# Gathering the rows of an expert layer by pairs of experts into two small buffers, and an eighth weight slot in place of the sorted array

## The reference, cut to what matters

```python
for i in range(DEPTH):                                  # DEPTH = 2
    h = rmsnorm(x, norm_mix[i])
    x = x + mixer(h, ...)                               # layer 0: sparse attention; layer 1: latent attention
    h = rmsnorm(x, norm_ffn[i]).reshape(512, 1024)
    x = x + hier_moe(h, ...)

def hier_moe(x2, ...):                                  # 512 tokens of 1024
    grp = argmax(softmax(x2 @ w_group + b_group))       # 1 of 8 groups
    top_p, top_i = top_k(softmax(logits of that group), 2)
    expert_id = grp * 8 + top_i                         # 2 of 64 experts for each token
    # rows sorted by expert: 1024 assignments, 16 for a mean expert
    y = (silu(xb @ w_gate[e]) * (xb @ w_up[e])) @ w_down[e]      # w_gate, w_up: 1024x256, w_down: 256x1024
    return for each token the weighted sum of its two rows of y
```

## Time and profile before

| what | value |
|---|---|
| median of 3 runs | 1631.71 us (1630.49 to 1633.06) |
| the profiled execution's own time | 1633.28 us |
| its span (first to last instruction) | 1631.5 us |
| TensorE busy | 1447.4 us, 89% |
| VectorE busy | 605.4 us, 37% |
| mean granted TensorE clock | 0.996 |
| experts, first up product of expert 0 to that of expert 60 | layer 0: 445.8 to 865.3 us; layer 1: 1160.3 to 1579.7 us |
| bytes moved by DMA | 480.67 MB, mean 295 GB/s |

### The profile page before, as it was taken

How to read it: one execution, slowest core, us unless ns; L and a number is a source line. 1 busy time by engine, 2 the same in 40 slices (tenths; PEclk the granted TensorE clock), 3 DMA queues, 4 the chain that set the end, 5 groups by cost and what they waited for, 6 DMA issues and landing times.

```text
span 1631.5 us, 24179 instructions
## 1 busy us (share of the span) xinstructions
PE 1447.4 (89%) x8991; PEld 903.8 (55%) x8991; DVE 605.4 (37%) x1517; ACT 341.0 (21%) x983; POOL 245.7 (15%) x290
## 2 busy tenths in 40 slices
PE   8999999999999988787878999999999977777785
PEld 3655466655566655454555555655666655555453
DVE  2145677752532221222213556423522222222225
ACT  2122377741110000000001345412100000000000
POOL 1122100000211111111112233000211111111112
PEclk9999999999999999999999999999999999999998
DMA  7115140026689999999999501473899999999997
GB/s 289 51 52 206 52 155 1 2 115 235 246 340 428 429 429 429 429 430 429 429 429 422 201 1 78 181 297 116 334 390 428 429 429 427 429 431 429 429 430 296
DMA packets 44373, 480.67 MB, mean 295 GB/s; under 512 B 11034, under 2 KB 11562, under 8 KB 24656
## 3 DMA queue, kind: packets, MB, share of 16 engines
q1 hardware_dynamic: 28144, 450.17, 65.9%
q0 software_dynamic: 15008, 25.37, 4.4%
q10 hardware_dynamic: 1152, 4.19, 0.6%
HBM read 461.33 MB, written 47.19 MB: 312 GB/s over the span
## 4 chain that ended last, share of the span: by engine, by line
PE 58%; DMA 32%; DVE 6%; issue 2%; ACT 1%; DVEq 0%; another core or an unknown queue 0%; POOL 0%; SPq 0%
DMA sb_arena<-moe_w 32%; PE ps L1173 12%; PE ps L1368 7%; PE ps L1583 7%; PE ps L1182 6%; PE ps L1689 2%; PE ps L1719 2%; PE ps L1704 2%; PE ps L1549 2%; PE ps L1409 2%; PE ps L1437 2%; PE ps L1433 1%; PE ps L1490 1%; PE ps L1520 1%; PE ps L1617 1%
## 5 line engine op out<-in xcount | busy, mean ns | idle before, releaser
L1173 PE MATMUL ps<-sb_arena,sb_x_block 128*64 128x256 f32 x4096 | 472.6, 383 | 91.5 <-DMA sb_arena<-moe_w 88.8
L1173 PEld LDWEIGHTS ps<-sb_arena,sb_x_block 128*64 128x64 f32 x4096 | 419.1, 197 | 198.6 <-issue 130.6
L1182 PE MATMUL ps<-sb_arena,sb_hidden_space 128*64 128x512 f32 x1024 | 247.9, 605 | 44.1 <-ACT sb_hidden_space L898 44.1
L768 POOL DMA_INDIRECT expert_rows<-sb_y_sb,sb_row_now x124 | 132.5, 1069 | 746.5 <-DVE sb_y_sb L1955 642.5
L1954 DVE COPY sb_row_now<-sb_row_of 128x1 uint32 (+1 forms) x124 | 19.1, 154 | 598.2 <-PE ps L1182 588.2
L898 ACT COPY sb_hidden_space<-ps 128x128 f32<-128x128 f32 x128 | 34.2, 267 | 755.8 <-PE ps L1248 755.8
L1182 PEld LDWEIGHTS ps<-sb_arena,sb_hidden_space 128*64 128x64 f32 x1024 | 62.1, 136 | 141.2 <-issue 73.1
L1368 PE MATMUL ps<-sb_sorted_rows,sb_arena 128*128 128x512 f32 x256 | 114.6, 594 | 2.1 <-DVE sb_arena L2199 1.3
L1965 DVE TENSOR_TENSOR sb_x_block<-sb_sorted_rows,sb_moe_gain 128x512 f32<-128x512 f32 x124 | 85.9, 693 | 25.0 <-issue 20.7
L1955 DVE COPY sb_y_sb<-ps 128x512 f32<-128x512 f32 x124 | 84.4, 681 | 0.0
L1368 PEld LDWEIGHTS ps<-sb_sorted_rows,sb_arena 128*128 128x128 f32 x256 | 46.9, 190 | 51.4 <-issue 48.8
(11 more groups left out here) (308 smaller groups left out, 1506.3 us busy)
## 6 DMA issues: line engine op xcount, KB each, us to landing
sb_arena<-moe_w SPq DMA_DIRECT2D x116, 3072.0 KB, 38.2
sb_arena<-moe_w SPq DMA_DIRECT2D x10, 2048.0 KB, 7.4
sb_arena<-moe_w SPq DMA_DIRECT2D x16, 1024.0 KB, 6.0
sb_sorted_rows<-nsa_w_group SPq DMA_DIRECT2D x2, 2048.0 KB, 13.2
sb_arena<-nsa_w_group SPq DMA_DIRECT2D x2, 2048.0 KB, 7.6
sb_sorted_rows<-nsa_w_out SPq DMA_DIRECT2D x1, 4096.0 KB, 13.9
kept_rows<-sb_arena SPq DMA_DIRECT2D x8, 512.0 KB, 4.9
token_rows<-sb_arena ACTq DMA_DIRECT2D x8, 512.0 KB, 2.7
```

Source lines behind the costliest of these rows:

```text
L768: pool.indirect_dma_start(out=ys_dram.rearrange("r (j n) -> (r j) n", j=2), out_offset=bass.IndirectOffsetOnAxis(ap=row_now[:, u:u + 1], a ...
L1173: last = nc.tensor.matmul(ps[j * BLOCK:(j + 1) * BLOCK, bank, 0:2 * P].rearrange("p (g n) -> p g n", g=2), x_rows[:, :, k], weights[:, 0:2 ...
L1182: last = nc.tensor.matmul(ps[j * BLOCK:(j + 1) * BLOCK, 2, :], hidT[:, c * BLOCK:(c + 1) * BLOCK], weights[:, 2, c * D + j * 512:c * D + ( ...
```

## The change

- `sorted_rows` no longer holds the rows. Its first part is weight slot 7 (`SLOTS = ARENA + 1 = 8`), its next part two buffers of 128 rows (`pair_rows`), each for one pair of experts: the 64 ranks of the even expert on partitions 0 to 63, those of the odd one on 64 to 127.
- Weight slot 7 is loaded by a third when the output projection has ended (`out_done`), and by two thirds after the last parts of slots 6 and 5.
- The list of tokens is by pair and rank: `token_of[p, q]` is the token of rank p % 64 of expert 2q + p // 64. Ranks come from the counting matmuls without `start`, tile by tile, and the one-hot matmuls of the first three tiles run during the routing. A missing rank gives 1000, out of bounds, and nothing is fetched for it.
- There are 32 indirect gathers of 128 descriptors of 4 KB instead of 8. The first two are issued when the list is ready. The gather of pair q + 2 waits for the turn of both blocks of pair q (the buffer) and stands in POOL's order between the row writes of expert 2q - 1 and expert 2q.
- TensorE turns the 64 rows of one expert with 8 transposes (`turn_block(n + 2)`) at the head of the iteration for expert n, ahead of `up(n + 1)`; an even one waits for its gather. `deal_block` reads the PSUM bank. The 16 copies into `xsT` go.
- The places in the sorted order (`start` plus rank) and the table for extra blocks are worked out after the first gathers; the router of the next layer is fetched after that table and ahead of the gather of pair 2.
- With over 64 rows for one expert, the extra blocks fetch their rows one by one. Neither layer's inputs need it.

```diff
-SLOTS = 7
+ARENA = 7
+SLOTS = ARENA + 1
...
-        xsT = sorted_rows[:, :].rearrange("p (n k) -> p n k", k=KD)
+        pair_rows = sorted_rows[:, SLOT:SLOT + 2 * D].rearrange("p (i n) -> p i n", i=2)
...
+        def slot_space(l, u):
+
+            return places(l, u) if u < ARENA else sorted_rows[:, 0:SLOT]
...
+                sp.wait_ge(out_done, OUT_PARTS * (l + 1))
+                part(ARENA, ARENA, 0, 1).then_inc(weights_loaded[ARENA], 16)
                 sp.wait_ge(last_rows_sent, 32 * (l + 1))
                 sp.wait_ge(logits_done, TILES * (l + 1))
                 part(RING + 2, RING + 2, 1, 3).then_inc(weights_loaded[RING + 2], 16)
                 part(RING + 1, RING + 1, 1, 2).then_inc(weights_loaded[RING + 1], 16)
+                part(ARENA, ARENA, 1, 3).then_inc(weights_loaded[ARENA], 16)
...
+                def gather(pair, j, tokens):
+                    pool.indirect_dma_start(
+                        out=pair_rows[:, j, :], out_offset=None, in_=h_dram,
+                        in_offset=bass.IndirectOffsetOnAxis(ap=tokens, axis=0),
+                        bounds_check=S - 1, oob_is_err=False).then_inc(pair_landed[j], 16)
+
+                pool.wait_ge(out_done, OUT_PARTS * (l + 1))
+                step(pool.memset(pair_rows, 0.0))
                 pool.wait_ge(token_ready, l + 1)
                 pool.wait_ge(first_rows_sent, 32 * (l + 1))
                 pool.wait_ge(last_rows_sent, 32 * (l + 1))
-                for c in range(CHUNKS):
-                    pool.indirect_dma_start(
-                        out=xs_in(c), out_offset=None, in_=h_dram,
-                        in_offset=bass.IndirectOffsetOnAxis(ap=token_of[:, c:c + 1], axis=0)).then_inc(rows_landed[c], 16)
+                for j in range(2):
+                    gather(j, j, token_of[:, j:j + 1])
 
                 pool.wait_ge(tables_ready, l + 1)
...
+                def send(i, u):
+                    pool.wait_ge(y_ready, i * 2 + (l * SENT + u + 1))
+                    pool.sem_inc(y_seen, 1)
+                    pool.indirect_dma_start(
+                        out=ys_dram.rearrange("r (j n) -> (r j) n", j=2),
+                        out_offset=bass.IndirectOffsetOnAxis(ap=row_now[:, u:u + 1], axis=0),
+                        in_=y_sb[:, u, :], in_offset=None, bounds_check=2 * ROWS - 1, oob_is_err=False
+                    ).then_inc(y_written[u], 16)
+
+                for j in range(2):
+                    pool.wait_ge(block_turned, base + 2 * j + 2)
+                    gather(j + 2, j, token_of[:, j + 2:j + 3])
                     for u in range(2):
-                        pool.wait_ge(y_ready, i * 2 + (l * SENT + u + 1))
+                        send(j, u)
+                step.enter(0, 2)
+                with pool.Fori(1, SENT_PAIRS // 2) as i:
+                    step.turn = i - 1
+                    for j in range(2):
+                        pool.wait_ge(block_turned, i * 4 + (base + 2 * j + 2))
                         pool.sem_inc(y_seen, 1)
+                        step(pool.tensor_copy(token_now[:, j:j + 1], token_of[:, bass.ds(i * 2 + (j + 2), 1)]))
+                        pool.sem_inc(y_seen, 1)
+                        gather(i * 2 + j + 2, j, token_now[:, j:j + 1])
+                        for u in range(2):
+                            send(i * 2 + j, u)
+                step.leave(SENT_PAIRS // 2 - 1)
+                for u in range(2):
+                    send(SENT_PAIRS - 1, u)
...
+                def turn_block(c, fours):
+                    half, i = c % 2, c // 2 % 2
+                    if half == 0:
+                        pe.wait_ge(pair_landed[i], (fours + (l * (EXPERTS // 4) + c // 4 + 1)) * 16)
+                        if not isinstance(fours, int):
+                            pe.sem_inc(y_seen, 1)
+                    turn_rows(half, i, TURN_BANK + half).then_inc(block_turned, 1)
+
+                turn_block(0, 0)
+                turn_block(1, 0)
+                keep_busy(1)
                 up(0, 0, 0)
...
+                for n in range(SLOTS):
+                    turn_block(n + 2, 0)
                     up(n + 1, n + 1, (n + 1) // SLOTS)
                     down(n, n)
+                turns = (SENT - 2) // SLOTS
+                with pe.Fori(1, turns) as i:
+                    for c in range(SLOTS):
+                        turn_block(c + 2, i * 2)
+                        up(i * SLOTS + (c + 1), c + 1, i + (c + 1) // SLOTS)
+                        down(i * SLOTS + c, SLOTS + c)
...
+                def deal_block(n, u):
+
+                    dve.wait_ge(block_turned, n + (base + 1))
+                    nc.vector.tensor_tensor(x_block[:, u].rearrange("p (a b) k -> p b a k", b=DEAL),
+                                            rows_by_column(TURN_BANK + u).rearrange("p (b a) k -> p b a k", b=DEAL),
+                                            moe_gain[:, l, :].unsqueeze(1).unsqueeze(1).to_broadcast([P, DEAL, BLOCK // DEAL, KD]),
+                                            ALU.mult).then_inc(block_ready, 1)
+
+                step.join()
+                deal_block(0, 0)
+                deal_block(1, 1)
+                extra_tables(l)
...
+            def mark_ranks(t):
+                v = nc.vector
+                step.join()
+                step(v.tensor_reduce(pos[:, :, t], ranked, AX, ALU.add))
+                v.tensor_tensor(rank_hot[:, t], col_no[:, 0:BLOCK].unsqueeze(1).to_broadcast([P, TOPK, BLOCK]),
+                                pos[:, :, t].unsqueeze(2).to_broadcast([P, TOPK, BLOCK]), ALU.is_equal).then_inc(hots_ready, 1)
```

359 lines of the change are left out of this document (177 added, 182 removed).

## The result

Median of 4 runs 1795.7 us (1790.3 to 1801.9) against 1631.6 us before (1630.5 to 1633.1): ratio 1.1007, 95% interval 1.0969 to 1.1044. The forecast was 1702 us, with 1725 as its upper end. The profiled execution took 1790.3 us, its span is 1787.9; rows are counted against the span of 1631.5 before. Three executions of the experiments (2928 us of `e_gather_early`, 4477 of `e_best`, 2986 of `e_small_start`), whose other executions agree within 0.4%, are left out of the medians and ratios.

What follows compares the result with a forecast made beforehand. Weight loads bound the stream at 7.46 us an expert; gather waits would make it 7.8, expert 60 34.9 us later plus 0.55 for a turn, twice 35.5 = 71 us: 1702 us, range 1672 to 1725 (0.60).

Steps and rivals of the forecast that it cites:

- The start: Layer start, token list to expert 0: list at 431.0, gather at 431.3, expert 0 at 439.4, 6.4 us earlier.
- The iteration: TensorE's work for one expert in the stream: 6.00 us plus 8 transposes at 0.55 us, 6.55 us.
- The landing L: Time from a stream gather's start to its landing: 14.9 us from above, 6.4 from below; break-even 12.9.
- The lower row: Stream gathers, some of whose packets meet no weight packet: 1.3 us less, 7.6 us an expert.
- the 7.8 us taken: Period of one expert in the stream with late gathers, chosen near the upper estimate of 7.95 us.
- A cycle of four experts: Stream loop from one down product through write, gather and turn to the next: 16.9 us plus the landing, if late.
- Hidden, but the rows lie badly: Rival: gathers not waited for, rows uneven over engines, 10.9 us more on half of them: 1647 us; chance 0.17.
- The writes behind the gathers hold `y_sb`: Rival: row writes behind gathers also delay `y_sb`, 8.0 to 8.2 us an expert, 1747 us; chance 0.05.
- Weights 3.4 us earlier by the slot: Rival: gathers hidden, weights set the pace, eighth slot brings them 3.4 us earlier a layer: 1625 us; chance 0.18.
- 16.9 + L: Price of four experts when the landing is late: 3.5 + L + 0.3 + 2 x 6.55.
- the upper row for L: Stream gathers, each packet waiting for one of weights, 0.90 us: L = 14.9, 7.95 us an expert.

Runs made afterwards that it cites:

- `e_gather_early`: Changed kernel, with the gather of pair q+2 issued between the writes of experts 2q-2 and 2q-1: 1729.0 us, ratio 1.0607.
- `e_best`: Changed kernel with earlier gather, both blocks of a pair turned together, every second slot's weights in two DMAs, no dummy product before the first up product: 1651.2 us.
- `e_small_start`: `e_best` plus ranks dealt over the 64 buffer rows, ten dummy products behind the token list, last loads ahead of the stream in 8 KB pieces: 1630.6 us.
- `e_pair_turns`: Changed kernel, with both blocks of a pair turned at once by 16 transposes alternating between the halves of the rows: 1787.0 us, ratio 1.0965.
- `e_thirds`: Changed kernel, with expert weights from the ninth on loaded by three DMAs of 8 KB a partition instead of one of 24 KB: 1668.6 us, ratio 1.0221.
- `e_no_rows`: Changed kernel, with every token list entry out of bounds, so that gathers move no rows: 1786.4 us, ratio 1.0983.
- `e_half_rows`: Changed kernel, with each gather fetching only the first 2 KB of its 4 KB rows: 1688.8 us, ratio 1.0353.
- `e_thirds_depth7`: `e_thirds`, with each load from the ninth expert on waiting for one expert more, so loads run seven deep: 1681.2 us, ratio 1.0302.
- `e_both_thirds`: Changed kernel with the earlier gather, turns by pairs and the stream's weights in three DMAs: 1662.3 us, ratio 1.0190.
- `b_thirds`: Kernel before the change, with weights of the experts from the eighth on loaded in three DMAs of a third each: 1647.5 us, ratio 1.0099.

## Why the prediction was wrong, by its own steps

The sign and the mechanism held, the range did not: +164 us against +71.

- **The start.** The first gather leaves at 429.5 instead of 431.3, but the landing took 9.15 us instead of 6.3, and expert 0 came at 442.3 instead of 439.4. The rows land 1.1 us later than forecast (429.52 + 9.15), and behind 4 us of idle time the sixteen transposes take 1.65 us instead of 1.1, and the dummy product ahead of expert 0, for which the forecast had no term, 2.07 us. +2.9 us in layer 0, and +5.6 between expert 60 of layer 0 and expert 0 of layer 1 (294.7 against 289.1 forecast).
- **The iteration: the first step that failed.** "8 transposes, 0.55 us" halved a row in which sixteen transposes took 1.10 us. Those sixteen alternated between two halves of the rows; eight of one half take 1.09 us by themselves, and `e_pair_turns` has sixteen in 1.10 us again. An iteration is 7.24, not 6.55 us: 0.54 of it are the turn, the rest mostly the up product behind it, which takes 3.67 us on the chain where the 6.00 us of the earlier trace rows had 3.45. With the first up product at the slower clock it costs 3 us over the first four experts, and two turns in each cycle of four experts bound by a landing, 2 x 0.54 = 1.1 us.
- **The landing L.** Taken between 14.9 and less, measured 15.1 (712.15 to 727.24). This term was right, and so was its making: turns of q0's packets with 24 KB packets, which `e_thirds`, `e_no_rows` and `e_half_rows` bear out. The lower row, in which some packets meet none, was given too much: the 7.8 us taken stand for an L of 14.3. The rule of the Trainium skill ("DMA: Bandwidth & Descriptors", section "Queues, rings and completion order") that an engine goes round its queues a packet at a time agrees (15.1 us behind 24 KB packets, no wait behind 8 KB ones); that a packet typically holds 9 to 17 descriptors doesn't hold for these gathers, where each row and each missing row is a packet of its own (18.9 packets a pair).
- **The clock: what the sum lacked.** After a wait of 4.6 us the granted clock is 0.50 and the next up product slow. By the page's groups it is 20 us a layer. The rows of before showed no such idle time in the stream (1.21 us ahead of an up product at full speed), and the forecast had no term for it. The Trainium skill has it ("TensorE: Matmul & The Clock Gate", section "HAM oscillation — how this bites in real kernels"): in a loop that waits for a DMA each time, each step starts at the slower clock. The trace agrees in the main, with 0.50 behind 4.6 us, but behind three of the 13 waits of layer 0 the up product has its 3.74 us.
- **The sum again.** A cycle of four experts was put at 31.2 us (4 x 7.8). With 1.1 for the turns and 20 / 14 = 1.4 for the clock it is 33.7; from expert 4 (469.4) to expert 60 (941.9) it is 472.5 / 14 = 33.75 us. That the two agree so well is partly luck: with the measured 15.1 us for L the same sum gives 16.9 + 1.1 + 1.4 + 15.1 = 34.5, and not every four experts hold a landing on the chain. Where they do, a cycle took 36.4 us (gathers at 831.60 and 868.00); where six experts lie between two of them, 50.8 (780.80 and 831.60). Counted without cycles, the 472.5 us are 56 iterations of 7.24 (405.4), 45.4 of waits for gathers and 20.5 by which ten up products exceed 3.74 us, 471.3 together; the forecast's 436.8 held 366.8 of iterations and 70 of waits. So the waits were put too high, and the iteration and the clock more than ate that up. In layer 0 expert 60 is 941.9 - 900.2 = 41.7 us later than forecast: 2.9 the start, 3.1 the first iterations, 35.7 the cycles. Layer 1: 5.6 ahead of expert 0, 36.0 up to expert 60, and 2.2 in the tail. Together 85.5 us on the span; the median of the runs lies 8 us over the span after, 0.1 before.
- **The rivals.** "Hidden, but the rows lie badly" was put at 10.9 us a layer on the busy engines; the deal gives 8 back, once the waits are out of the way. "The writes behind the gathers hold `y_sb`" isn't what the changed kernel does, where VectorE waits for TensorE, and its price, 8.2 us, would have been near the 8.4 measured for another reason; but it is what appears as soon as the gather is moved ahead of a write. "Weights 3.4 us earlier by the slot" has no run of its own: the 6.3 us a layer of `e_thirds_depth7` are the price of a stream that starts one expert later.

The step by which the range failed is thus the cycle's price, 16.9 + L: 16.9 should have been 18.0, since the eight transposes were put at 0.55 us and take 1.09, and the clock's 1.4, put at nothing, come on top. With both corrected, the upper row for L would have stood at 8.6 us an expert; measured are 8.4.

How far the design comes is shown by the last two kernels. With the ranks dealt, the gathers ahead of the second write, turns by pairs, some weights in halves and TensorE kept busy at the start, the changed design comes out level with the kernel before (0.9995, 0.9986 to 1.0004), and no version beat it that fetches its rows. The DMA engines are full in the stream in both; that what the slot and the earlier start give is taken by rows in the stream and smaller packets is the likely account, not measured as a sum.

Open: why the first gather of a layer takes 8.5 to 10 us; why some short waits are followed by a slow up product and others not; and how the 15 us of `e_both_thirds` divide between single engines, which the records don't show. The clock's price in the changed kernel is summed from rows; only at the layer's start was idle time taken away by an experiment (2.4 us for two layers, with intervals that just overlap).

## What to carry to other kernels

In this kernel a small transfer beside a full queue paid by the packet, not by the byte. Count the packets of all its neighbours for one period against those of the big queue, and multiply by the time of one big packet, before asking when a buffer comes free. If the small queue has more packets in a period than the big one (19 against 16 here), earlier issue helps only in part (1795.7 to 1729.0 us); smaller big packets (8 or 12 KB) remove the wait, fewer small ones shorten it. Don't take half of a measured group of instructions for half its time when the group alternates between two halves of the rows, and price each wait of some microseconds on TensorE with the slower clock behind it.

## What the runs showed of the hardware

- A descriptor past the bounds still costs a turn: gathers without any row, 4 bytes a descriptor in the packet records, were about as late as full ones (20 landings on the chain, 14.2 to 15.7 us but for one of 12.4; 1786 against 1796 us).
- Two neighbouring descriptors of 2 KB, or of nothing, share a packet, those of 4 KB rows don't, with a row or without.
- Eight 64-row transposes of one half take as long (1.09 us) as sixteen that alternate between the halves (1.10 us).
- Weights in packets of 8 KB instead of 24 KB take 3% more of the engines' time: 99.0% of 250 us for 103.18 MB in `b_thirds`, 0.960% a MB, against 98.1% for 105.16 MB before, 0.933%.
- Idle times of 4.6 and 5.05 us were followed by a granted clock of 0.50 and 0.63; 0.93 us of idle time was not. Idle times of 1.03 us (`e_small_start`, layer 1, 5.42 us) and 1.99 us (the change, 762.19, 4.95 us) had a slow up product behind them, others of 1.22 (`e_small_start`, layer 0) and 1.95 us (the change, 595.34) did not.
- Where the rows of a gather lie in SBUF changes the time by 16 us for the same bytes, number of packets and order (1662.3 against 1646.5).
